# Convolution taps and LayerNorm stages moved two slots forward, divisions moved by half a slot, one LN2 spread in pieces, in a one-layer streaming encoder on one core

## What is computed

```python
proj = x @ w_in                       # q, k, v and 2*512 columns for the convolution
attn = window attention(q, k, v)      # partial rotary, 128-token band, sinks in the softmax
c_in = u[..., :512] * sigmoid(u[..., 512:])
c = causal depthwise conv(c_in, 31 taps)
c = silu(_layer_norm(c, conv_ln_g, conv_ln_b))              # "cln"
h = _layer_norm(ALPHA * x + concat([attn, c]) @ w_out, ...)  # "ln1"
up = h @ w_up                         # 2 * 2816 columns
upc = causal depthwise conv(up, 3 taps)
f = (silu(upc[..., :2816]) * upc[..., 2816:]) @ w_down
ple = sigmoid(h @ w_pg + b_pg) * (p @ w_pe)
y = _layer_norm(ALPHA * h + f + ple, ln2_g, ln2_b)          # "ln2"
```

## Time and profile before

| | us |
|---|---|
| median of 3 runs (2437.03 to 2440.82) | 2437.51 |
| the profiled execution's own time | 2435.67 |
| its span, first to last instruction | 2433.9 |
| PE busy | 2373.3 (98%) |
| DVE / ACT / POOL busy | 1466.8 / 1277.4 / 1601.6 |
| granted TensorE clock, mean | 0.991 of full speed |

### The profile page before, as it was taken

How to read it: one execution, slowest core, us unless ns; L and a number is a source line. 1 busy time by engine, 2 the same in 40 slices (tenths; PEclk the granted TensorE clock), 3 DMA queues, 4 the chain that set the end, 5 groups by cost and what they waited for, 6 DMA issues and landing times.

```text
span 2433.9 us, 38834 instructions
## 1 busy us (share of the span) xinstructions
PE 2373.3 (98%) x15081; PEld 2335.4 (96%) x15081; DVE 1466.8 (60%) x2375; ACT 1277.4 (52%) x2083; POOL 1601.6 (66%) x1284
## 2 busy tenths in 40 slices
PE   7999999999999999999999999999999999998997
PEld 7898999999999999999999999999999999998997
DVE  6757883666766267766536766663576665374432
ACT  4556655555444456644444664445465444466653
POOL 8477887765665776566577656557775665777874
PEclk9999999999999999999999999999999999999999
DMA  6244445443333544333344433334443333535443
GB/s 239 97 145 150 165 160 177 163 138 119 120 123 106 168 158 139 123 118 121 110 166 156 147 114 117 123 115 157 153 156 122 116 127 104 174 131 182 165 144 104
DMA packets 119094, 341.54 MB, mean 140 GB/s; under 512 B 15360, under 2 KB 43648, under 8 KB 118912
## 3 DMA queue, kind: packets, MB, share of 16 engines
q1 hardware_dynamic: 98256, 312.89, 38.3%
q10 hardware_dynamic: 20656, 26.17, 3.3%
HBM read 330.12 MB, written 8.99 MB: 139 GB/s over the span
## 4 chain that ended last, share of the span: by engine, by line
PE 86%; DVE 6%; ACT 3%; POOL 2%; DMA 2%; issue 1%; ACTq 0%; DVEq 0%
PE ps L591 28%; PE ps L593 27%; PE ps L592 27%; POOL w_lo L538 2%; DVE sq L1303 1%; DMA w_raw<-in_panels 1%; PE ps L649 1%; ACT w_hi L767 1%; PE ps L680 1%; DVE acc L1240 1%; PE ps L668 1%; PE ps L658 1%; DVE u_out L1168 0%; DVE u_out L1166 0%; PE ps L695 0%
## 5 line engine op out<-in xcount | busy, mean ns | idle before, releaser
L538 POOL TENSOR_TENSOR w_lo<-w_raw,w_hi 128x512 fp32r<-128x512 f32 (+1 forms) x1272 | 1600.6, 1286 | 802.5 <-ACT w_hi L767 796.3
L767 ACT CAST w_hi<-w_raw 128x1024 fp32r<-128x1024 f32 (+2 forms) x635 | 621.5, 981 | 596.4 <-PE ps L593 410.3
L591 PE MATMUL ps<-h_hi,w_hi 128*128 128x386 f32 (+5 forms) x2496 | 815.6, 327 | 7.7 <-DVE f_lo L1181 4.3
L592 PE MATMUL ps<-h_lo,w_hi 128*128 128x386 f32 (+5 forms) x2496 | 807.0, 323 | 0.0
L593 PE MATMUL ps<-h_hi,w_lo 128*128 128x386 f32 (+5 forms) x2496 | 806.9, 323 | 0.0
L591 PEld LDWEIGHTS ps<-h_hi,w_hi 128*128 128x128 f32 x2496 | 473.2, 190 | 15.5 <-issue 8.4
L592 PEld LDWEIGHTS ps<-h_lo,w_hi 128*128 128x128 f32 x2496 | 473.7, 190 | 1.4
L593 PEld LDWEIGHTS ps<-h_hi,w_lo 128*128 128x128 f32 x2496 | 473.9, 190 | 0.0
L591 PE MATMUL ps<-f_hi,w_hi 128*128 128x384 f32 (+2 forms) x1264 | 412.1, 326 | 7.0 <-POOL w_lo L538 4.4
L592 PE MATMUL ps<-f_lo,w_hi 128*128 128x384 f32 (+2 forms) x1264 | 406.5, 322 | 0.0
L593 PE MATMUL ps<-f_hi,w_lo 128*128 128x384 f32 (+2 forms) x1264 | 406.5, 322 | 0.0
(11 more groups left out here) (153 smaller groups left out, 2021.7 us busy)
## 6 DMA issues: line engine op xcount, KB each, us to landing
w_raw<-in_panels SPq DMA_DIRECT2D x540, 512.0 KB, 3.2
w_raw<-in_panels SPq DMA_DIRECT2D x48, 384.0 KB, 3.0
w_raw<-in_panels SPq DMA_DIRECT2D x48, 128.0 KB, 2.3
xres<-in_xT ACTq DMA_DIRECT2D x32, 192.0 KB, 2.7
out_yT<-res ACTq DMA_DIRECT2D x4, 1536.0 KB, 6.4
a_raw<-in_xT ACTq DMA_DIRECT2D x6, 768.0 KB, 6.7
x_raw<-in_xT SPq DMA_DIRECT2D x2, 768.0 KB, 6.7
xres<-in_pT ACTq DMA_DIRECT2D x8, 192.0 KB, 3.3
```

The source lines that it names most:

```text
L538: ins = pool.tensor_tensor(w_lo[:, n % WS, c], w_raw[:, n % RS, c], w_hi[:, n % WS, c].bitcast(F32), ALU.subtract)
L591: pe.matmul(out, w_hi[:, sl, c], hi, start=first, stop=False)
L592: pe.matmul(out, w_hi[:, sl, c], lo, start=False, stop=False)
L767: act.copy(w_hi[:, n % WS, 0:w], w_raw[:, n % RS, 0:w]).then_inc(w_hi_done, 1)
```

## The change

Four things are done, all in the order of stages and none in the arithmetic.

1. For tiles 2 to 5 the convolution taps are spread over slots 0 to 21 (before: 0 to 24), and each stage of their "cln" comes two slots earlier: `tree` in slot 23, `root` in 27, `scale` in 28, `affine` and `high` in 29, `lo` in 30.
2. For tile 1 all 32 steps of channel block 0 are done before the slots of tile 0: between the stages of the first LayerNorms, behind the `out` groups and behind the last `in` groups. Channel 1 starts in slot 0. "cln" 1 stands as in 1. `first_norm` is cut in two on DVE, with five taps between.
3. `divide` of tile 1's three units stands behind the first group of its slot instead of behind the second.
4. LN2 of tile 4 works in four pieces of two blocks; its multiply is spread over slots 4 and 5 and its affine over slots 5, 6 and 7 of tile 5, where the transfer to `yT` also goes.

```diff
+SPREAD = (("ln2", LAST - 1),)
@@ mix_at
-                if k == 1 + 4 * u + n:
+                if k == 1 + 4 * u + n and (name, t) != ("divide", 1):
...
-        taps = {8: (1, 4)}
-        taps.update({n: (0, 4) for n in range(8)})
-        taps.update({n: (1, 7) for n in range(9, 13)})
-        taps.update({n: (2, 4) for n in range(13, 21)})
-        taps.update({n: (3, 8) for n in range(21, 25)})
+        if t == 1:
+            counts = {1: [4] * 8, 2: [3, 6, 6, 6, 6, 5], 3: [4, 4, 4, 4, 3, 3, 3, 7]}
+        else:
+            counts = {0: [5, 5, 5, 5, 6, 6], 1: [5, 5, 5, 8, 9], 2: [8, 8, 5, 5, 6], 3: [5, 5, 5, 5, 5, 7]}
...
-        for name, n in (("tree", 25), ("mean", 26), ("centre", 26), ("square", 27), ("sqtree", 28), ("var", 29),
-                        ("root", 29), ("scale", 30), ("affine", 31), ("high", 31), ("lo", 32)):
+        for name, n in (("tree", 23), ("mean", 24), ("centre", 24), ("square", 25), ("sqtree", 26), ("var", 27),
+                        ("root", 27), ("scale", 28), ("affine", 29), ("high", 29), ("lo", 30)):
@@ before the slots of tile 0
     stage("conv_add", 0, 3)
+    stage("conv_in", 1, 0)
...
     stage("first_norm")
+    stage("taps", 1, 0, 5)
+    stage("first_scale")
...
+            if i == 0:
+                stage("taps", 1, 0, (1, 2, 1, 1, 1, 4, 4, 2)[m])
...
+            stage("taps", 1, 0, 3)
...
+            if i == 0 and n in (1, 2, 4):
+                stage("taps", 1, 0, {1: 3, 2: 3, 4: 2}[n])
@@ the slots
-        late = {0: ("mean", "centre"), 1: ("square",), 2: ("sqtree",), 4: ("var", "root", "scale"), 5: ("affine",)}
+        late = {0: [("mean",), ("centre",)], 1: [("square",)], 2: [("sqtree",)], 4: [("var",), ("root",), ("scale", 0, 1)],
+                5: [("scale", 2, 3), ("affine", 0)], 6: [("affine", 1, 2)], 7: [("affine", 3)]}
...
-            stage("conv_in", i + 1, 0)
+            stage("conv_in", i + 1, 0 if i else 1)
...
+                if i == 0 and g == two_groups[0] and k in (2, 6, 10):
+                    stage("divide", 1, k // 4)
@@ scale (DVE); affine (ACT) takes its pieces in the same way
-                for b in pieces(name, t):
+                for n in some or range(len(parts)):
+                    b = parts[n]
                     dve.tensor_tensor(z[:, b, :], z[:, b, :], std.unsqueeze(1).broadcast_to([P, b.stop - b.start, w]), ALU.mult
                                       ).then_inc(scaled, 1)
@@ taps (DVE)
                 if first == 0:
+                    own.wait()
                     dve.wait_ge(conv_in, n + 1)
```

More of the change, by code:

```diff
@@ L66 @@
 CONV_BANK, AUX = 5, 6
-RUNNING = tuple(("ln1", t) for t in (LAST,))
+RUNNING = (("ln1", LAST),)
+SPREAD = (("ln2", LAST - 1),)
 def plan():
@@ L87, in mix_at @@
             stage("att_split", t)
-        taps = {8: (1, 4)}
-        taps.update({n: (0, 4) for n in range(8)})
-        taps.update({n: (1, 7) for n in range(9, 13)})
-        taps.update({n: (2, 4) for n in range(13, 21)})
-        taps.update({n: (3, 8) for n in range(21, 25)})
-        if k in taps:
+        if t == 1:
+            counts = {1: [4] * 8, 2: [3, 6, 6, 6, 6, 5], 3: [4, 4, 4, 4, 3, 3, 3, 7]}
+        else:
+            counts = {0: [5, 5, 5, 5, 6, 6], 1: [5, 5, 5, 8, 9], 2: [8, 8, 5, 5, 6], 3: [5, 5, 5, 5, 5, 7]}
+        taps = [(c, n) for c, some in counts.items() for n in some]
+        starts = {n: taps[n + 1][0] for n in range(len(taps) - 1) if taps[n + 1][0] != taps[n][0]}
+        if k < len(taps):
             stage("taps", t, *taps[k])
-        if k in (7, 12, 20):
-            stage("conv_in", t, {7: 1, 12: 2, 20: 3}[k])
-        for name, n in (("tree", 25), ("mean", 26), ("centre", 26), ("square", 27), ("sqtree", 28), ("var", 29),
-                        ("root", 29), ("scale", 30), ("affine", 31), ("high", 31), ("lo", 32)):
+        if k in starts:
+            stage("conv_in", t, starts[k])
+        for name, n in (("tree", 23), ("mean", 24), ("centre", 24), ("square", 25), ("sqtree", 26), ("var", 27),
+                        ("root", 27), ("scale", 28), ("affine", 29), ("high", 29), ("lo", 30)):
             if k == n:
@@ L221, in plan @@
             else:
-                for name in late.get(k, ()):
-                    stage(name, "ln2", i - 1)
+                for name, *some in late.get(k, ()):
+                    stage(name, "ln2", i - 1, *some)
     for m in range(KB):
@@ L268, in pieces @@
 def pieces(name, t):
-    return PIECES if (name, t) in RUNNING else [slice(0, HB if name == "cln" else KB)]
+    return PIECES if (name, t) in RUNNING + SPREAD else [slice(0, HB if name == "cln" else KB)]
 END = signals(LAST_NO)
@@ L973, in high, with affine @@
                 act.copy(hi, z).then_inc(hi_done, 1)
-            def affine(name, t):
+            def affine(name, t, *some):
                 z, hi, lo, nb, w = ln_of(name, t)
@@ L980, in affine @@
                     load_functions(func)
-                for n, b in enumerate(pieces(name, t)):
+                parts = pieces(name, t)
+                for n in some or range(len(parts)):
+                    b = parts[n]
                     act.wait_ge(scaled, before + n + 1)
@@ L989, in affine @@
                         act.copy(hi[:, b, :], z[:, b, :]).then_inc(hi_done, 1)
-                if name != "ln2":
+                if name != "ln2" or n < len(parts) - 1:
                     return
-                act.wait_ge(affine_done, signals(LN_NO[name, t]) + 1)
+                act.wait_ge(affine_done, before + len(parts))
                 y = O["yT"].rearrange("(b p) t -> p b t", p=P)
@@ L1353, in square_sums, with scale @@
                 tree(sq[:, :, 0:w], nb, w, sqsum_done)
-            def scale(name, t):
+            def scale(name, t, *some):
                 z, hi, lo, nb, w = ln_of(name, t)
-                dve.wait_ge(std_done, LN_NO[name, t] + 1)
                 std = ps[:, AUX + 1, 0:w]
-                own.step(dve.reciprocal(std, std))
-                own.wait()
-                dve.wait_ge(centred, signals(LN_NO[name, t]) + len(pieces(name, t)))
-                for b in pieces(name, t):
+                parts = pieces(name, t)
+                if not some or some[0] == 0:
+                    dve.wait_ge(std_done, LN_NO[name, t] + 1)
+                    own.step(dve.reciprocal(std, std))
+                    own.wait()
+                    dve.wait_ge(centred, signals(LN_NO[name, t]) + len(parts))
+                for n in some or range(len(parts)):
+                    b = parts[n]
                     dve.tensor_tensor(z[:, b, :], z[:, b, :], std.unsqueeze(1).broadcast_to([P, b.stop - b.start, w]), ALU.mult
@@ L1378, in first_norm, with first_scale @@
                     dve.tensor_tensor(z, z, ps[:, AUX, 0:w], ALU.subtract).then_inc(centred, 1)
+            def first_scale():
+                w = WIDTH[0]
                 dve.wait_ge(std_done, 1)
@@ L1466, in _ @@
                     first_norm()
+                elif what == "first_scale":
+                    first_scale()
                 elif what == "last_norm":
```

## The result

| | before | changed |
|---|---|---|
| median, us (22 runs each) | 2435.93 (2431.24 to 2440.82) | 2438.72 (2435.61 to 2445.36) |
| ratio, 95% interval | | 1.0012 (1.0006 to 1.0017) |
| span of the profiled execution, us | 2433.9 | 2440.1 |

The changed kernel is 2.8 us slower, by the interval 1.5 to 4.1 us. Forecast were 2428 us and a range from 2420 to 2436, so the time lies outside of the range and on the slow side of before. The profiled executions differ by 6.2 us, more than the medians do. So the traces tell where stalls stand, and the timed ratios tell what they are worth.

What follows compares the result with a forecast made beforehand. PE, busy 98% of the span, was the bound; only its idle time and slow clock could give. The terms summed to 9.3 us gained: 2435.67 to 2426.4, plus 1.8 for the median, 2428 us; range 2420 to 2436.

Steps and rivals of the forecast that it cites:

- Step 1: Tile 1's two transposes: of 3.7 us of PE stalls 1.0 stays; gain 2.7, and 1.7 for the clock.
- the stalls only change their place: Rival: DVE and ACT hold the pace, stalls return one slot on; 2434 to 2438 us, no change; chance 0.22.
- Step 2: Before part 1 of `d`, PE's 2.31 us wait for pair 15's `f_lo` shrinks by 0.5, plus 1.7 for the clock.
- Step 3: Slot 26 of tile 0: DVE does both `p_split` and `sqtree`, so PE newly waits before `var`; loss 1.4 us.
- Step 4: `pg` slots: 8.3 us of stalls and clock go, a new 3.9 stall at `pg` 2 and 1.7 clock come; gain 2.7.
- All of it goes: Claim that PE's two starved waits in the `pg` slots, 4.9 us, and 3.4 of slow clock vanish, 8.3 us.
- Step 5: LN2 of tile 4, in tile 5: one 5.2 us stall before `d 5 0 0` replaces three of 6.6; gain 1.4.
- Step 6: Taps before the slots and the wider tiles 1 to 4: no stall of theirs touched, counted at nothing.
- the slower rival: Wide tiles get the `pg` 2 stall: 3 us with 1.7 of slow clock in each of tiles 1 to 3; 2442; chance 0.06.

## Why the prediction was wrong

**The mechanisms stood, the balance didn't.** Of the signs that the prediction named, all but one came: no stall before the two transposes (0.59 and 0.43 us stand before the `mixed` matmuls behind them), a wait for `sq` before `var` (2.47, 1.4 forecast), one of 4.27 us before `pg` 2 for `f_lo` (3.9 forecast), one of 4.94 before `d` 5 0 0 (5.2 forecast), no stall in the wide tiles. The one that failed is "no wait for POOL in the `pg` slots". The error of 10.7 us against the changed kernel's median is 9.3 of gain forecast and 2.8 of loss measured, less 1.6 by which the base was too high, and 0.2 of rounding. Its parts:

- **Step 1, the divisions** (forecast -4.4 us, measured alone -1.2). The stall left was 0.59 + 0.43, where 1.0 was forecast. The step failed behind it: it said what may be late next, `mixed` and the next unit, and did not go on to the groups behind. `d` 0 0 0 with its `f_lo` 7 is the third group behind the second transpose, and its margin was below zero already: PE waited 0.30 us for it before. A stall of 0.30 is a flag that says that there is no slack. In the changed kernel's trace the sum lacks 2.67 us of stall and 3.1 for the 6.8 us at half clock, of which PE worked 6.2. The rival "the stalls only change their place" named this and had 0.22.
- **Step 2, the taps ahead of part 1 of `d`** (forecast -2.2). Stall 1.23 where 1.8 was forecast, clock up behind it. Right, and a little better.
- **Step 3, the wait before `var`** (forecast +1.4, bounds 0 to 1.8; 2.47 in five traces of five). The sum took 2.85 us for `sqtree` from its old place; behind `p_split` it takes 3.58, which is 0.7 of the 1.1 us that the term was short. And a stall of this size was charged no clock, though the prediction's own opening said that a stall of 2 can cost nearly 4: 3.4 us at half speed stand behind it in all five. Taking the stall out alone was worth 2.7 us, with 2.5 to either side.
- **Step 4, "cln" 1 out of the `pg` slots** (forecast -2.7, with step 3 -1.3; putting the LayerNorm back gave -5.6, so together they cost +5.6). This is the main error, 6.9 us. The new stall at `pg` 2 was sized well. The mistake is "All of it goes" for POOL's two stalls: the block was moved, not removed. It still keeps the weights' casts and transfers back for 5.7 us, and PE waits for POOL again before `pg` 5 and 7, 0.83 + 2.75 = 3.58 us, with a half clock of its own (the stretch from 400.50). Before, such waits made 5.27 us (1.90, 2.99 and 0.38), so 1.7 us of them went and not 4.9. The clock term was wrong on both sides. The credit of 3.4 us took the whole stretch of 6.7 us, but by the earlier trace rows PE worked only 4.07 of it and stood still for the rest, and a slow clock costs nothing while PE stands still: the stretch was worth 2.0. The charge of 1.7 stands against two stretches, behind `pg` 2 and behind `pg` 7, worth 1.4 and 1.7.
- **Step 5, LN2** (forecast -1.4, measured +0.2). PE came with one stall of 4.94, as worked out, and a small one of 0.32 before it; the half clock behind it lasts 6.8 us, not 3.4, and PE works 5.6 of them. With that the step is 6.6 + 1.5 = 8.1 against 5.3 + 2.8 = 8.1: nothing, as measured. The interval of the measurement (1.9 faster to 2.4 slower) holds the forecast too.
- **Step 6 and the wide tiles.** At nothing, and the runs don't contradict it; the slower rival (a stall in tiles 1 to 3) did not happen.
- **The base.** 1.8 us were added for the median of three runs. Over 22 runs the median of before is 2435.93, so the profiled execution was a typical one and the addition was the noise of three.

The same steps, filled with what the two traces show. Each stretch of half clock counts with half of the time that PE was busy in it. The column "PE moved" is what the starts of groups say for the same part (from `u` 0 0 to `d` 0 0 7, to `u` 0 34, to `out` 1 0, and from `u` 5 10 to `d` 5 1 0):

| step | stalls, us | clock, us | sum | PE moved | forecast |
|---|---|---|---|---|---|
| 1 | -3.7 + 1.0 + 2.7 | -1.7 + 3.1 | +1.4 | +1.0 | -4.4 |
| 2 | -1.1 | -1.7 | -2.8 | -2.7 | -2.2 |
| 3 | +2.5 | +1.7 | +4.2 | with 4 | +1.4 |
| 4 | -5.3 + 4.3 + 3.6 | -2.0 + 1.4 + 1.7 | +3.7 | +7.7 (3 and 4) | -2.7 |
| 5 | -6.6 + 5.3 | -1.5 + 2.8 | 0.0 | 0.0 | -1.4 |

Part by part the sums come within 0.4 us of what PE's starts say. They make +6.5, the two spans differ by 6.2, and outside of these parts PE gained 0.7 us before the first slot and lost 0.9 in the wide tiles. So the list of places accounts for these two executions. The forecast credited every stall that goes in full, with its clock, and charged those that come in part. Against the timed kernels the table is too high, at step 1 by 2.6 (1.4 against -1.2) and at steps 3 and 4 by 2.3 (7.9 against 5.6), each about as large as the interval, and the timed change is +2.8. That a part of the half clock of these two traces is not in every execution would explain it (below), but was not shown for these places.

The Trainium skill ("ScalarE: Activation LUTs", section "What ACT_TABLE_LOAD costs") would have made the stall at `pg` 2 5.3 us instead of 3.9. It measured 4.27, and in the rows above the sigmoid starts at 375.43 behind a load of 1.28 that starts at 374.13: no drain beyond the load is seen.
